# Rotary partners as rows of a unit's two tiles, against a permutation matmul

## The reference

```python
def rope_1d(x, pos):
    half = x.shape[-1] // 2
    ...
    x1, x2 = xf[..., :half], xf[..., half:]
    return jnp.concatenate([x1 * cos - x2 * sin, x2 * cos + x1 * sin], axis=-1).astype(x.dtype)

def rope_2d(x):
    t = jnp.arange(x.shape[1])
    n = x.shape[-1] // 2
    return jnp.concatenate([rope_1d(x[..., :n], t // GRID_W), rope_1d(x[..., n:], t % GRID_W)], axis=-1)
```

## Time and profile before

| what | value |
|---|---|
| time, median of 3 runs | 4072.53 us (4071.81 to 4072.68) |
| time of the profiled execution | 4076.61 us |
| its span, first to last instruction | 4074.9 us |
| mean granted TensorE clock | 0.977 |
| TensorE busy | 3845.0 us (94%) |
| VectorE busy | 2099.4 us (52%) |
| ScalarE busy | 916.3 us (22%) |
| GpSimd busy | 558.4 us (14%) |

### The profile page before, as it was taken

One profiled execution on the slowest core, in us unless ns is written; L12 is line 12 of the kernel. 1 busy time (PEld: TensorE's weight loads), 2 busy tenths in 40 slices (PEclk: granted clock), 3 DMA queues, 4 the chain that ended last, 5 costly groups with the idle time before them and its releaser, 6 DMA issues. The chain is left out here.

```text
span 4074.9 us, 47294 instructions
## 1 busy us (share of the span) xinstructions
PE 3845.0 (94%) x18444; PEld 2989.6 (73%) x18444; DVE 2099.4 (52%) x3442; ACT 916.3 (22%) x1718; POOL 558.4 (14%) x432
## 2 busy tenths in 40 slices
PE   6898999889999999999989989999999999999998
PEld 4787556565888888888868855566568888888886
DVE  5222555555476666665572245555546545454445
ACT  3111455443210000000031125544512000000002
POOL 0011011101211111111131101110022111111112
PEclk8999999999999999999999989999999999999999
DMA  6754223564122122112215433256440100110011
GB/s 228 224 186 127 65 54 80 140 144 145 43 83 63 47 73 73 54 56 73 63 51 183 137 82 83 50 125 138 106 166 32 42 32 32 42 42 32 32 42 52
DMA packets 289646, 358.53 MB, mean 88 GB/s; under 512 B 102994, under 2 KB 215508, under 8 KB 289296
## 3 DMA queue, kind: packets, MB, share of 16 engines
q1 hardware_dynamic: 269008, 350.54, 29.5%
q10 hardware_dynamic: 20416, 4.98, 0.6%
HBM read 288.28 MB, written 72.16 MB: 88 GB/s over the span
## 5 line engine op out<-in xcount | busy, mean ns | idle before, releaser
L2056 PE MATMUL bank<-h_hi,w_hi 128*128 128x512 f32 (+1 forms) x2496 | 905.4, 363 | 21.1 <-issue 14.7
L2057 PE MATMUL bank<-h_lo,w_hi 128*128 128x512 f32 (+1 forms) x2496 | 886.2, 355 | 0.0
L2058 PE MATMUL bank<-h_hi,w_lo 128*128 128x512 f32 (+1 forms) x2496 | 886.0, 355 | 0.0
L2210 PE MATMUL bank<-prob,vv 128*128 128x512 f32 (+3 forms) x1504 | 703.7, 549 | 0.0
L1874 DVE SCALAR_TENSOR_TENSOR xT<-bank,mods,xT 128x512 f32<-128x512 f32 (+1 forms) x816 | 536.8, 661 | 321.9 <-PE bank L2058 305.2
L2056 PE MATMUL bank<-m_hi,w_hi 128*128 128x512 f32 (+1 forms) x1536 | 569.8, 371 | 53.1 <-DVE xT L1874 51.3
L2056 PEld LDWEIGHTS bank<-h_hi,w_hi 128*128 128x128 f32 x2496 | 472.7, 189 | 103.5 <-issue 33.8
L2058 PE MATMUL bank<-m_hi,w_lo 128*128 128x512 f32 (+1 forms) x1536 | 547.0, 356 | 0.0
L2057 PE MATMUL bank<-m_lo,w_hi 128*128 128x512 f32 (+1 forms) x1536 | 546.0, 355 | 0.0
L2057 PEld LDWEIGHTS bank<-h_lo,w_hi 128*128 128x128 f32 x2496 | 472.8, 189 | 73.4 <-issue 7.7
L2058 PEld LDWEIGHTS bank<-h_hi,w_lo 128*128 128x128 f32 x2496 | 472.6, 189 | 66.7
(11 more groups left out here) (187 smaller groups left out, 4080.7 us busy)
## 6 DMA issues: line engine op xcount, KB each, us to landing
stage<-in_w_mlp SPq DMA_DIRECT2D x64, 1024.0 KB, 5.2
nx_w<-in_w_ada SPq DMA_DIRECT2D x16, 1536.0 KB, 9.2
stage<-in_w_in SPq DMA_DIRECT2D x18, 1024.0 KB, 6.3
ada_h<-in_w_ada SPq DMA_DIRECT2D x16, 1024.0 KB, 7.9
rope_t<-in_k_rope SPq DMA_DIRECT2D x28, 512.0 KB, 4.4
k<-s_kB SPq DMA_DIRECT2D x48, 224.0 KB
k<-s_kA SPq DMA_DIRECT2D x24, 448.0 KB, 10.5
k<-s_kD SPq DMA_DIRECT2D x24, 448.0 KB, 10.7
```

The costliest lines, as they stand in the source:

```text
L2056: x = pe.matmul(out, a_hi, b_hi, start=first, stop=False)
L2057: pe.matmul(out, a_hi, b_lo, start=False, stop=False)
L2058: return x, pe.matmul(out, a_lo, b_hi, start=False, stop=last)
L2210: pe.matmul(ob[:, q0:q0 + n], vv[h % 2][:, key0 // P], prob[si % NP_RING][:, :n], start=(i == 0 and kind != "D"), stop=(i == len(steps) - ...
```

## The change

For units 3, 4 and 7 the columns of w_in are put in another order on the host, so that a column and its rotary partner are the same row of the unit's two tiles m = 0 and m = 1. The rotation of either tile then reads the other tile's bank directly, and needs no permutation matmul; the sign of the sine differs between the tiles and becomes VectorE's factor. Both tiles use the same table, which is loaded once for the pair. B's half width is 8 and D's is 16, so a store to scratch, which must put the rows back in their own order, writes runs of 8 or 16 rows with gaps. Unit 8, with a single tile of keys, keeps the matmul.

- SP: the table is loaded for m = 0 only (8 loads a layer instead of 14); the stores of the three units have an access pattern of three dimensions.
- TensorE: 2 permutations a layer instead of 14; before group i it now also waits, where group i-4 is such a rope group, for the product that reads group i-4's bank for its partner.
- VectorE: `rp1` is a scalar_tensor_tensor from the partner's bank, which waits for the partner's `zf`.
- ScalarE: `zf` has no wait for a permutation and no scale (the scale of D's queries is in their table); the copy `xn` of unit 4 is made in two instructions that put the columns back in order.
- GpSimd: takes the same table for both tiles.

```diff
+def natural_column(d, m, r):
+
+    half = d // 4
+    return r // half * (2 * half) + m * half + r % half
...
-    rope = np.zeros((2, 2, P, LAT), np.float32)
+    rope = np.zeros((3, 2, P, LAT), np.float32)
...
+    rope[1] *= np.float32(QS)
...
+ROTATED = {3: 32, 4: 32, 7: HD}
...
+        _g["load"] = _g["unit"] not in ROTATED or _g["m"] == 0
+        _l += _g["load"]
+        _g["li"] = _l - 1
+        if _g["unit"] not in ROTATED:
+            _g["si"] = _s
+            _s += 1
+    if _g["unit"] in ROTATED and _g["form"] in ("t", "rope"):
+        _g["partner"] = _i + 1 - 2 * _g["m"]
...
                     for part, src in ((0, z_hi[s]), (1, z_lo[s])):
-                        sp.dma_start(dst[part, row:row + P, g["col"]:g["col"] + g["n"]],
-                                     src[:, :g["n"]].bitcast(F32)).then_inc(z_out[s], 16)
+                        rows = dst[part, row:row + P, g["col"]:g["col"] + g["n"]]
+                        if g["unit"] in ROTATED:
+                            half, width = ROTATED[g["unit"]] // 4, dst.shape[-1]
+                            rows = bass.AP(tensor=dst.tensor, offset=(part * 256 + g["m"] * half) * width + g["col"],
+                                           ap=[[2 * half * width, P // half], [width, half], [1, g["n"]]])
+                        sp.dma_start(rows, src[:, :g["n"]].bitcast(F32)).then_inc(z_out[s], 16)
...
-                if g["form"] == "rope":
-                    r = g["ri"]
-                    if r == 0:
+                if g.get("load"):
+                    x = g["li"]
+                    if x == 0:
...
-                    sp.wait_ge(rp_1, l * NR + r + 1)
-                    sp.wait_ge(rp_2, l * NR + r + 1)
-                    kd = 0 if g["kind"] == "B" else 1
-                    sp.dma_start(rope_t[r % 2], I["k_rope"][kd, :, :, g["c"] * 512:(g["c"] + 1) * 512].rearrange(
-                        "s p n -> p s n")).then_inc(rope_in[r % 2], 16)
+                    if l or x >= 2:
+                        last = [y["ri"] for y in GROUPS if y.get("li") == (x - 2) % NTAB][-1]
+                        sp.wait_ge(rp_1, (l - (x < 2)) * NR + last + 1 + CREDIT)
+                        sp.wait_ge(rp_2, (l - (x < 2)) * NR + last + 1 + CREDIT)
+                    sp.dma_start(rope_t[x % 2], I["k_rope"][g["table"], :, :, g["c"] * 512:(g["c"] + 1) * 512].rearrange(
+                        "s p n -> p s n")).then_inc(rope_in[x % 2], 16)
...
-                    act.wait_ge(rp_full, l * NR + r + 1)
+                    swaps = sum(1 for x in GROUPS if x.get("si") is not None and x["ri"] <= r - 2)
+                    if l or swaps:
+                        act.wait_ge(rp_full, l * NSWAP + swaps)
                     act.wait_ge(rp_2, l * NR + r + 1)
-                    act.activation(zf[r % 2], src, ACT.Copy, scale=g["scale"]).then_inc(zf_rdy, 1)
+                    act.activation(zf[r % 2], src, ACT.Copy).then_inc(zf_rdy, 1)
...
-                    act.activation(xn[x % 2], src, ACT.Copy).then_inc(xn_rdy, 1)
+                    if g["unit"] in ROTATED:
+                        half = ROTATED[g["unit"]] // 4
+                        for t in range(2):
+                            cols = slice(t * UW, (t + 1) * UW)
+                            copied = act.activation(xn[x % 2][:, cols].rearrange("p (w h i) -> p h w i", h=2, i=half),
+                                                    src[:, cols].rearrange("p (h w i) -> p h w i", h=2, i=half), ACT.Copy)
+                        copied.then_inc(xn_rdy, 1)
...
-                    dve.tensor_tensor(rp1, bank[:, 4 + r % 2], rope_t[r % 2][:, 1], ALU.mult).then_inc(rp_1, 1)
+                    if "partner" in p:
+                        x = GROUPS[p["partner"]]
+                        dve.wait_ge(zf_rdy, l * NR + x["ri"] + 1)
+                        settle(dve)
+                        dve.wait_ge(rope_in[t % 2], l * R_USES[t % 2] * 16 + (t // 2 + 1) * 16)
+                        dve.scalar_tensor_tensor(out=rp1, in0=bank[:, x["i"] % 4], scalar=1.0 if p["m"] else -1.0, in1=sine,
+                                                 op0=ALU.mult, op1=ALU.mult).then_inc(rp_1, 1)
...
                     if p["form"] == "rope":
                         pe.wait_ge(zf_rdy, l * NR + p["ri"] + 1)
+                        if "partner" in p:
+                            settle(pe)
+                            pe.wait_ge(rp_1, l * NR + GROUPS[p["partner"]]["ri"] + 1 + CREDIT)
...
                 in_group(g)
-                if GROUPS[g["i"] - 1]["form"] == "rope":
+                if "si" in GROUPS[g["i"] - 1]:
                     swapped(GROUPS[g["i"] - 1])
...
+    for u, d in ROTATED.items():
+        order[u * UW:(u + 1) * UW] = [u * UW + natural_column(d, m, r) for m in range(2) for r in range(P)]
+    arrays["w_in"] = np.ascontiguousarray(arrays["w_in"][..., order])
```

More of the change, by code:

```diff
@@ L64, in constants @@
     c["headsum"] = (i[:, None] // HD == i[None, :] // HD).astype(np.float32)
-    c["swap"] = np.stack([(i[:, None] == (i[None, :] ^ 8)), (i[:, None] == (i[None, :] ^ 16))]).astype(np.float32)
+    c["swap"] = (i[:, None] == (i[None, :] ^ 16)).astype(np.float32)
     ang = 2.0 * np.pi * np.outer(np.arange(HD), np.arange(HD)) / HD
@@ L79, in constants @@
                                                         np.full((P, 1), fold[1, 0, 0])], 1))
-    rope = np.zeros((2, 2, P, LAT), np.float32)
+    rope = np.zeros((3, 2, P, LAT), np.float32)
     t = np.arange(LAT)
-    for kind, d in enumerate((32, HD)):
+    for table, (d, part) in enumerate(((32, 1), (HD, 1), (HD, None))):
         n = d // 2
@@ L86, in constants @@
         for r in range(P):
-            j = r % d
+            j = r % d if part is None else natural_column(d, part, r) % d
             pos = (t // GRID_W) if j < n else (t % GRID_W)
             a = pos.astype(np.float32) * inv[j % half]
-            rope[kind, 0, r] = np.cos(a)
-            rope[kind, 1, r] = np.sin(a) * (-1.0 if j % n < half else 1.0)
+            rope[table, 0, r] = np.cos(a)
+            rope[table, 1, r] = np.sin(a) * (-1.0 if j % n < half else 1.0)
+    rope[1] *= np.float32(QS)
     c["rope"] = rope
@@ L297 @@
 _t = _r = _n = _v = _x = 0
+_s = _l = 0
 for _i, _g in enumerate(GROUPS):
@@ L316 @@
         _r += 1
+        _g["table"] = {3: 0, 4: 0, 7: 1}.get(_g["unit"], 2)
+        _g["load"] = _g["unit"] not in ROTATED or _g["m"] == 0
[6 more added lines that the diff above has]
+        _g["partner"] = _i + 1 - 2 * _g["m"]
 NG, NT, NR, NN, NTURN, NX_IN = len(GROUPS), _t, _r, _n, _v, _x
+NSWAP, NTAB = _s, _l
 _h = 0
@@ L396 @@
 N_USES = [sum(1 for i in range(NN) if i % 2 == b) for b in range(2)]
-R_USES = [sum(1 for i in range(NR) if i % 2 == b) for b in range(2)]
+R_USES = [sum(1 for i in range(NTAB) if i % 2 == b) for b in range(2)]
 UNITS_AT = [(0, 1, 2, 3), (0, 1, 2, 3), (2, 0, 3, 1)]
@@ L466, in trunk @@
     headsum = put("headsum", [P, P])
-    swap = put("swap", [P, 2, P])
+    swap = put("swap", [P, P])
     pair = put("pair", [P, 2])
@@ L877, in _ @@
             load_bias_row(n, ada_in[n])
-        for dst, src in ((headsum, I["k_headsum"]), (swap, I["k_swap"].rearrange("s p n -> p s n")),
+        for dst, src in ((headsum, I["k_headsum"]), (swap, I["k_swap"]),
                          (fin_a[:, :, 0], I["final_g"].rearrange("(k p) -> p k", p=P))):
@@ L1202, in turned @@
                 pool.wait_ge(zf_rdy, l * NR + r + 1)
-                pool.wait_ge(rope_in[r % 2], l * R_USES[r % 2] * 16 + (r // 2 + 1) * 16)
+                x = g["li"]
+                pool.wait_ge(rope_in[x % 2], l * R_USES[x % 2] * 16 + (x // 2 + 1) * 16)
                 pool.wait_ge(zr_rdy, l * NR + r + 1)
-                pool.tensor_tensor(rp2[r % 2], zf[r % 2], rope_t[r % 2][:, 0], ALU.mult).then_inc(rp_2, 1)
+                pool.tensor_tensor(rp2[r % 2], zf[r % 2], rope_t[x % 2][:, 0], ALU.mult).then_inc(rp_2, 1)
             for g in GROUPS:
@@ L1378, in evacuate @@
                         act.wait_ge(xn_out[x % 2], l * X_ALL[x % 2] + X_OUT[x - 2])
-                    act.activation(xn[x % 2], src, ACT.Copy).then_inc(xn_rdy, 1)
+                    if g["unit"] in ROTATED:
[5 more added lines that the diff above has]
+                        copied.then_inc(xn_rdy, 1)
+                    else:
+                        act.activation(xn[x % 2], src, ACT.Copy).then_inc(xn_rdy, 1)
                 elif g["form"] == "n":
@@ L1685, in evacuate @@
                     r = p["ri"]
-                    dve.wait_ge(rp_full, l * NR + r + 1 + CREDIT)
-                    dve.wait_ge(rope_in[r % 2], l * R_USES[r % 2] * 16 + (r // 2 + 1) * 16)
-                    dve.tensor_tensor(rp1, bank[:, 4 + r % 2], rope_t[r % 2][:, 1], ALU.mult).then_inc(rp_1, 1)
+                    t = p["li"]
+                    sine = rope_t[t % 2][:, 1]
+                    if "partner" in p:
[5 more added lines that the diff above has]
```

(13 more changed lines are left out.)

## The result

The change made the kernel slower: 4086.63 us median of 5 runs (4080.83 to 4095.16) against 4072.53 us, a ratio of 1.0042 with a 95% interval of 1.0029 to 1.0054 (the two medians alone are 14.1 us apart, 0.35%). My forecast was 4060.3 us, with 4068 as the upper end of its range. The profiled execution took 4080.83 us with a span of 4079.2. It is the fastest of the five, and only 4.2 us longer than the one profiled before. So I compare stretches of the two traces, not their totals.

The account below looks back on a forecast made before the run. TensorE, busy for 94% of the span, was taken as the bound. Unit 7's 6.9, g37's 2.8 and 4.0, less 1.5 for the clock, made 12.2 us: 4072.5 becomes 4060.3 us, range 4051 to 4068.

Parts of the forecast that it names:

- I take 2.6, since a row is 2 KB either way: Stores of units 3, 4 and 7: with gaps they land in 2.6 us, between bounds of 2.5 and 8.0 us.
- a landing beyond 4 us: Gapped stores: one of the stated signs that the prediction is wrong; about 2.6 us was expected.
- while unit 7's stores stay hidden: Unit 7's stores: by the skill's rule they would use half the engines, with the sum unchanged if hidden.
- The rival that held the truth: Gapped stores land late, moving three links a layer; slower by 0.2% from D = 3.4 us, up to 4093 us; 5%.
- Unit 7: 6.9 us: Unit 7: four permutations fewer a layer count whole, 3.46 us a layer, 6.9 us for both.
- g37 sooner by 2.8 and 4.0 us: Units 3 and 4: the chain to g37 shortens by 2.8 us in the first layer, 4.0 in the second.
- `w_lo` at 2.28 us: VectorE, units 5 and 6: `w_lo` would take 2.28 us, where some had taken 3.36 and 3.38 us.
- products of a pair together: GpSimd: with one table for the pair, its two products would run back to back.
- g30's wait: TensorE at g30: a new wait of 1.25 us for VectorE's product of g27, swallowed by the wait at g37.
- eight permutation matmuls left: TensorE: the profile after would show 8 permutation matmuls in place of 56.
- The clock: TensorE from g37: 5.2 us of idling brings the low clock in the first layer too, 1.5 us lost.
- my 12.2: Whole kernel: the forecast gain in us, 6.9 + 2.8 + 4.0 - 1.5.

Follow-up runs that it names:

- a_plain_stores: Changed kernel, but the stores of units 3, 4 and 7 write 128 consecutive rows again: 4066.34 us, ratio 0.9991.
- b_gapped_stores: Kernel before, with only the stores of units 3, 4 and 7 written with gaps as in the change: 4076.74 us, ratio 1.0012.
- a_d16: Changed kernel, with D's columns reordered so that unit 7's stores have 16 as outermost dimension in place of 8: 4075.88 us, ratio 1.0009.
- a_rows: Changed kernel, unit 7's stores with 16 outermost, and units 3 and 4's stores to every second row with one stride: 4065.92 us, ratio 0.9987.
- a_pool_apart: Changed kernel, but GpSimd's product of a pair's second tile waits for VectorE's addition of the first tile: 4085.81 us, ratio 1.0037.
- a_tables_early: Changed kernel with its gapped stores, but each rope table issued some groups sooner: 4083.72 us, ratio 1.0031.
- a_lo_apart: Changed kernel, with VectorE making `w_lo` of units 5 and 6 later, in the turns of g30 and g38: 4085.38 us, ratio 1.0036.

## Why the prediction was wrong

- **The stores: the step that failed.** "I take 2.6, since a row is 2 KB either way" was wrong for both shapes, by 0.5 us to landing in B (2.7 against 2.2 us, 232.84 to 235.56 after, 234.86 to 237.05 before) and by 2.5 to 2.9 us in D, and every issue costs SP 0.2 us more. a_plain_stores puts the sum at 20 us, of the 26 by which I missed. The prediction's own sign of being wrong, a landing beyond 4 us, came true in D. I had the reason for D in hand, the Trainium skill's rule on the outermost dimension, and wrote that it would change nothing "while unit 7's stores stay hidden". They had been hidden behind the permutations that the same change removes: b_gapped_stores shows the cover, a_plain_stores its loss. a_d16 shows that the dimension of 8 is D's cause. For B, whose outermost dimension is 16, that rule of the Trainium skill gives no loss; one stride in place of two levels brings it back (a_rows), and why a second level costs landing time too stays open.
- **The rival that held the truth** had 5% and a price by landings alone, even at first only from D = 2.0 us. In B the landing grew by much less than that. It moved the table behind g31's stores by the landing alone, and left out the issues on SP's queue, the table's own time behind such stores (5.5 us for 4.05) and unit 7.
- **Unit 7: 6.9 us.** The term is right with good stores: 3.5 us a layer in a_plain_stores, a_d16 and a_rows. With the stores of the change it was -0.7 a layer.
- **g37 sooner by 2.8 and 4.0 us.** Counted from g23, it came 5.6 and 1.6 us later. With good stores (a_rows) it came 0.85 and 2.5 sooner. The table of links tells why in the first layer: the table of g31 lands 2.75 us sooner (47.75 to 45.00), as the prediction has it, and 1.1 of that is lost by g33 and another 1.1 by `w_lo` of unit 6. Each time `zr` takes about 1.0 us more, because GpSimd's two products now run back to back, the second beside VectorE's addition. I had seen the price in the second layer (1.83 us beside GpSimd) and counted on the products' moving away from there; they moved onto `zr`, which is in the chain as well. This share is read from the rows of a_rows; a_pool_apart, which tested it with the slow stores in place, doesn't show it in the time. The chain also had a wrong last link at g31, its table: a_tables_early shows GpSimd's `w_hi` and the 1 MB load there. Load and table are issued one behind the other and moved together, so the forecast for that link came out by luck.
- **`w_lo` at 2.28 us, products of a pair together, g30's wait, eight permutation matmuls left:** right in kind. g30's wait was 3.93 and 2.34 us for 1.25, and 1.38 and 1.72 in a_rows: most of the excess is the stores'. **The clock:** low at g37 in both layers, as told, and also at g30, which wasn't.
- **The sum with good stores.** a_rows is 6 us faster for my 12.2. Its two layers, g12 to attention, are shorter by 2.4 and 3.5 us: unit 7 gives 3.5 each, g37 gives 0.85 and 2.5, 1.7 and 0.4 are lost from g37 to g60, the low clock's among them, 1.4 of the second layer ahead of g23, and the rest behind g75.

## What to carry to other kernels

When work comes off the bound engine, ask what was hidden behind that same work, and price everything in its stretch as if it had no cover. A layout that moves a permutation into a store's pattern isn't free: look at the outermost dimension and the number of levels of the pattern, and try for one stride. And after such a change, the order written for the old timing has to be set again: here that was worth 8.5 us more than the repaired change by itself.

## What the runs showed of the hardware

- A 256 KB store of 128 rows of 2 KB took 2.1 to 2.4 us from the issue of its `z_lo` part to the release of the writer that waited for it with one stride, whether rows are adjacent or every second one (232.32 to 234.41 in a_rows), 2.6 to 3.5 us with two levels and 16 outermost (3.5 in a_lo_apart, 228.61 to 232.10), and 4.85 to 5.1 us with 8 outermost.
- Its issue mostly took SP 0.32 us (`z_hi`) and 0.43 us (`z_lo`) with one stride, and 0.52 to 0.60 us with two levels.
- VectorE's addition of two f32 tiles of 128x512 took 0.69 us alone and 1.70 us beside a product on GpSimd (222.62). The three-operand form that reads a bank of PSUM and a table didn't slow down: it took 0.69 us at 221.12, with GpSimd's first product running from 221.22 (all in the kernel after). The same form on two tiles of SBUF, `z_lo`, did: 1.33 us at 227.05 in a_pool_apart, beside GpSimd's product from 226.52.
